# Places of their own for the first block's modulation pieces, and four top-sixteen units under the latents' queries

## The reference

```python
def first_block(x, c, ...):
    c_act = jax.nn.silu(c)
    for l in range(DEPTH):                                   # DEPTH = 2
        mod = c_act @ w_ada[l] + b_ada[l]                    # [1024] @ [1024, 6144]
        sh_m, sc_m, gt_m, sh_f, sc_f, gt_f = jnp.split(mod[:, None, :], N_MOD, axis=-1)
        h = rms_norm(x, g_pre_mix[l]) * (1.0 + sc_m) + sh_m
        y = token_mixer(h, w_in[l], ...)                     # h @ w_in: [256,1024] @ [1024,3656]
        x = x + gt_m * rms_norm(y, g_post_mix[l])
        h = rms_norm(x, g_pre_ffn[l]) * (1.0 + sc_f) + sh_f
        y = conv_glu_ffn(h, w_up_act[l], w_up_lin[l], ...)   # [256,1024] @ [1024,2816], twice
        x = x + gt_f * rms_norm(y, g_post_ffn[l])

def peer(h, w_q, subkeys, u, v):        # 8 heads, 2 halves of 128 keys each, per 128 tokens
    q = (xb @ w_q).reshape(PEER_BLOCK, PEER_HEADS, 2, PEER_DHALF)
    s = jnp.einsum('thpd,hpkd->thpk', q, subkeys)
    s1, i1 = lax.top_k(s[:, :, 0], 16); s2, i2 = lax.top_k(s[:, :, 1], 16)
    cand = s1[..., :, None] + s2[..., None, :]
    top, pos = lax.top_k(cand, 16)
    g = jax.nn.softmax(top, axis=-1)
    ue, ve = u[idx], v[idx]             # a gathered row is 2 x 1024 floats
    act = jax.nn.gelu(jnp.einsum('td,thkd->thk', xb, ue))
    return jnp.einsum('thk,thkd->td', g * act, ve)
```

## Time and profile before

| | us |
|---|---|
| median of 3 runs (lowest to highest) | 3843.72 (3842.69 to 3852.66) |
| profiled execution, its own time | 3842.15 |
| its span, first to last instruction | 3840.9 |
| PE busy | 3050.1 (79%) |
| DVE busy | 2455.0 (64%) |
| ACT, POOL busy | 784.2 (20%), 940.7 (24%) |
| mean granted TensorE clock | 0.909 |
| HBM | 287 GB/s over the span |

### The profile page before, as it was taken

The page is one execution under the profiler, slowest core; times in us unless marked ns, Lnnn a source line. Parts: engine busy times, 40 slices in busy tenths (PEclk is TensorE's granted clock), DMA queues, the critical chain, the costliest instruction groups (busy, mean ns, idle before and its releaser), DMA issues. The chain is left out here.

```text
span 3840.9 us, 28366 instructions
## 1 busy us (share of the span) xinstructions
PE 3050.1 (79%) x8769; PEld 1590.1 (41%) x8769; DVE 2455.0 (64%) x5374; ACT 784.2 (20%) x1876; POOL 940.7 (24%) x842
## 2 busy tenths in 40 slices
PE   6898797899786799787767777777897787777776
PEld 1354464675334377254344223322343462233322
DVE  3224556887677488646656999766514519999665
ACT  1102223232224433225211111100102211111000
POOL 0000001222221233222302344434100013444432
PEclk7999898999898899888879998999996799999999
DMA  6654234999795689966847999999632059999998
GB/s 236 201 178 167 93 114 169 343 356 354 301 356 199 230 349 406 373 248 212 306 154 294 391 388 389 392 422 422 257 138 103 21 206 367 386 389 376 422 421 348
DMA packets 194025, 1102.15 MB, mean 287 GB/s; under 512 B 22517, under 2 KB 22849, under 8 KB 95569
## 3 DMA queue, kind: packets, MB, share of 16 engines
q0 software_dynamic: 114512, 818.87, 54.1%
q1 hardware_dynamic: 78736, 280.90, 20.2%
q10 hardware_dynamic: 624, 0.57, 0.1%
HBM read 1099.18 MB, written 1.05 MB: 286 GB/s over the span
## 5 line engine op out<-in xcount | busy, mean ns | idle before, releaser
L2022 PE MATMUL PS<-AR 128*128 128x512 f32 x2464 | 1216.7, 639 | 400.7 <-DVE AR L2064 341.2
L2121 POOL DMA_INDIRECT AR<-in_uv,AR x768 | 866.1, 1128 | 1641.9 <-PE PS L2022 1142.8
L2069 DVE CUSTOM_DVE_ANT_0 AR<-AR 128x1024 f32<-128x1024 f32 x768 | 935.6, 1220 | 297.2 <-DMA AR<-in_uv,AR 296.7
L2022 PEld LDWEIGHTS PS<-AR 128*128 128x128 f32 x2464 | 476.1, 202 | 1103.3 <-DVE AR L2064 536.5
L694 PE MATMUL PS<-AR 128*128 128x512 f32 (+3 forms) x1304 | 565.3, 588 | 27.4 <-DMA AR<-in_w_in 14.7
L2034 ACT ACTIVATE AR<-AR 128x2 f32<-128x2 f32 x384 | 78.1, 203 | 1514.8 <-DVE AR L2069 1509.2
L694 PEld LDWEIGHTS PS<-AR 128*128 128x128 f32 x1304 | 250.5, 205 | 314.9 <-issue 269.5
L991 PE MATMUL PS<-AR 128*128 128x256 f32 x1408 | 327.2, 392 | 22.9 <-DMA AR<-in_w_up_act 11.9
L326 DVE SCALAR_TENSOR_TENSOR AR<-AR,CC 128x512 f32<-128x512 f32 x280 | 210.5, 752 | 208.5 <-DMA AR<-in_w_ada 130.7
L991 PEld LDWEIGHTS PS<-AR 128*128 128x128 f32 x1408 | 273.2, 196 | 85.0 <-issue 17.4
L1941 PE MATMUL PS<-AR 128*128 128x256 f32 x768 | 186.7, 406 | 26.7 <-DMA AR<-in_peer_w_q 19.6
(11 more groups left out here) (226 smaller groups left out, 2490.3 us busy)
## 6 DMA issues: line engine op xcount, KB each, us to landing
AR<-in_w_mod SPq DMA_DIRECT2D x96, 512.0 KB, 4.3
AR<-in_w_ada SPq DMA_DIRECT2D x96, 512.0 KB, 4.6
AR<-in_w_in SPq DMA_DIRECT2D x56, 512.0 KB, 4.0
AR<-in_peer_w_q SPq DMA_DIRECT2D x48, 512.0 KB, 3.3
AR<-in_w_up_act SPq DMA_DIRECT2D x44, 512.0 KB, 7.7
AR<-in_w_up_lin SPq DMA_DIRECT2D x44, 512.0 KB, 7.5
AR<-in_w_down SPq DMA_DIRECT2D x44, 512.0 KB, 9.6
AR<-in_even_w_in SPq DMA_DIRECT2D x24, 512.0 KB, 4.2
```

What stands on the lines that cost most here:

```text
L2022: ins = pe.eng.matmul(acc[i][hh], e.dg(x), e.buf(x)[:, 1024 + 512 * hh:1536 + 512 * hh], start=(x == e.on[False][i][0]), stop=(x == e.on[F ...
L2069: v.eng.tensor_tensor_reduce(e.buf(x)[:, 0:1024], e.buf(x)[:, 0:1024], norm2(e).H[e.tiles[x // 128]], 1.0, 0.0, ALU.mult, ALU.add, DT[x // ...
L2121: g.eng.indirect_dma_start(e.buf(x), None, D["uv"][e.l], bass.IndirectOffsetOnAxis(ap=idx_at(x // 16, x % 16, 1), axis=0)).then_inc(*land. ...
```

## The change

Three lists of places are added: `OWN_T`, three of 128x512 in the area `t`; `OWN_BIG`, three in `big`; `ACM`, two in `acc`. With `own` given, `Mods` loads each 128x512 half by a DMA of its own (256 KB) into the next of the three places; the DMA waits for DVE's use of the half that lay there, and the first three wait for the `guard`, which is the turned norm that has read the area before. The three modulations named above get `own`. `more` sums in `ACM` in place of `ACW`. For the latents' experts, `ready` no longer holds `more`, and `begin, under` go from 11, 1 to 3, 4.

```diff
+        OWN_T = [T[:, a:a + 512] for a in (1536, 3072, 3584)]
+        OWN_BIG = [BIG[:, 5632 + 512 * i:6144 + 512 * i] for i in range(3)]
+        ACM = [area("acc")[:, 512 * i:512 * i + 512] for i in range(2)]
...
             def sp(self, sp):
+                place, n = {}, len(self.own)
                 for j, hh, outs in self.halves:
                     r = 2 * j + hh
                     for kh in range(4):
-                        load(sp, ("raw", self.key, j, hh, kh), self.w[r, kh].rearrange("p (c n) -> p c n", c=2),
-                             2, 512, [("piece", self.key, j, hh, kh)])
+                        if n:
+                            for c in range(2):
+                                i = self.nth(j, hh, kh, c) % n
+                                sp.wait_ge(place.get(i, self.guard))
+                                sp.eng.dma_start(self.own[i], self.w[r, kh, :, 512 * c:512 * c + 512]).then_inc(
+                                    *land.landed(f"own{i}", "raw", self.key, j, hh, kh, c))
+                                place[i] = ("piece", self.key, j, hh, kh, c)
+                        else:
+                            load(sp, ("raw", self.key, j, hh, kh), self.w[r, kh].rearrange("p (c n) -> p c n", c=2),
+                                 2, 512, [("piece", self.key, j, hh, kh)])
                         yield
...
+                        wt = self.columns(j, hh, kh, c)
+                        v.wait_ge(v.last, ("raw", self.key, j, hh, kh, c) if self.own else ("raw", self.key, j, hh, kh))
...
-                mods_of["first", 0] = ada("ada0b", 0, (2, 4, 3, 5), AF, {0: n1r, 1: n1r}, n1t)
+                mods_of["first", 0] = ada("ada0b", 0, (2, 4, 3, 5), AF, {0: n1r, 1: n1r}, n1t, OWN_T)
...
-                mods_of["next", 0] = ada("ada1a", 1, (1, 0, 2), AF, {0: n2r, 1: n2r, 2: [("added", 0, 2)]}, n2t)
+                mods_of["next", 0] = ada("ada1a", 1, (1, 0, 2), AF, {0: n2r, 1: n2r, 2: [("added", 0, 2)]}, n2t, OWN_BIG)
...
-                                         (0, [(1, 0, "shift", None), (2, 4, "shift", None)])], ACW,
+                                         (0, [(1, 0, "shift", None), (2, 4, "shift", None)])], ACM,
...
-                          mods.finished() + [("sum", before, 255)], 11, 1)
-                  for l, mods, before in ((0, more, "c"), (1, mods_of["odd"], "l0"))]
+                          [("sum", before, 255)] + mods, 3, 4)
+                  for l, mods, before in ((0, [], "c"), (1, mods_of["odd"].finished(), "l0"))]
```

More of the change, by code:

```diff
@@ L262, in program, with __init__ @@
         class Mods:
-            def __init__(self, key, w, row0, jobs, accs, frees, guard=(), every=1):
+            def __init__(self, key, w, row0, jobs, accs, frees, guard=(), every=1, own=()):
+                self.own = own
                 self.key, self.row0, self.jobs, self.accs = key, row0, jobs, accs
@@ L283, in sp, with nth, columns @@
                     for kh in range(4):
-                        load(sp, ("raw", self.key, j, hh, kh), self.w[r, kh].rearrange("p (c n) -> p c n", c=2),
-                             2, 512, [("piece", self.key, j, hh, kh)])
+                        if n:
[8 more added lines that the diff above has]
+                                 2, 512, [("piece", self.key, j, hh, kh)])
                         yield
                 yield
+            def nth(self, j, hh, kh, c):
+                return 8 * [h[:2] for h in self.halves].index((j, hh)) + 2 * kh + c
+            def columns(self, j, hh, kh, c):
+                if self.own:
+                    return self.own[self.nth(j, hh, kh, c) % len(self.own)]
+                return raw_view(2, 512, "raw", self.key, j, hh, kh)[:, c, :]
             def pool(self, g):
@@ L312, in piece @@
                 j, hh, outs = self.halves[q]
-                wt = raw_view(2, 512, "raw", self.key, j, hh, kh)
                 for n, (ci, dst, kind, gain) in enumerate(outs):
@@ L320, in piece @@
                             ("acc", self.key, j, hh, n) if c == 1 and kh == 3 else ())
-                        v.wait_ge(v.last, ("raw", self.key, j, hh, kh))
+                        if self.own:
+                            end = ("piece", self.key, j, hh, kh, c)
+                        wt = self.columns(j, hh, kh, c)
+                        v.wait_ge(v.last, ("raw", self.key, j, hh, kh, c) if self.own else ("raw", self.key, j, hh, kh))
                         if kc == 0:
                             v.wait_ge(("silu",), self.acc_before(q, n))
-                            v.eng.tensor_scalar(acc, wt[:, c, :], col, None, ALU.mult).then_inc(*v.done(*end))
+                            v.eng.tensor_scalar(acc, wt, col, None, ALU.mult).then_inc(*v.done(*end))
                         else:
-                            v.eng.scalar_tensor_tensor(out=acc, in0=wt[:, c, :], scalar=col, in1=acc, op0=ALU.mult,
+                            v.eng.scalar_tensor_tensor(out=acc, in0=wt, scalar=col, in1=acc, op0=ALU.mult,
                                                        op1=ALU.add).then_inc(*v.done(*end))
@@ L358, in out_pe @@
                         bk = bank(pe, SIDE, *key)
-                        pe.wait_ge(("piece", self.key, j, hh, 3), ("acc", self.key, j, hh, n)
+                        pe.wait_ge(("piece", self.key, j, hh, 3, 1) if self.own else ("piece", self.key, j, hh, 3), ("acc", self.key, j, hh, n)
                                    if n < len(outs) - 1 else None)
@@ L857, in ada_rows, with ada @@
                     4: (1, "scale", D["g_pre_ffn"][l]), 3: (0, "shift", None), 5: (3, "gate", D["g_post_ffn"][l])}[j]
-        def ada(key, l, js, accs, frees, guard=()):
-            return Mods(key, D["w_ada"][l], 12 * l, [(j, [(0, *ada_rows(j, l))]) for j in js], accs, frees, guard)
+        def ada(key, l, js, accs, frees, guard=(), own=()):
+            return Mods(key, D["w_ada"][l], 12 * l, [(j, [(0, *ada_rows(j, l))]) for j in js], accs, frees, guard,
+                        own=own)
         def rope(v, x1, x2, c, s, r):
@@ L2458, in program @@
             if l == 0:
-                mods_of["first", 0] = ada("ada0b", 0, (2, 4, 3, 5), AF, {0: n1r, 1: n1r}, n1t)
+                mods_of["first", 0] = ada("ada0b", 0, (2, 4, 3, 5), AF, {0: n1r, 1: n1r}, n1t, OWN_T)
             else:
-                mods_of["first", 1] = ada("ada1b", 1, (4, 3, 5), AF, {0: n1r, 1: n1r, 3: [("added", 0, 3)]}, n1t)
+                mods_of["first", 1] = ada("ada1b", 1, (4, 3, 5), AF, {0: n1r, 1: n1r, 3: [("added", 0, 3)]}, n1t, OWN_T)
             n2 = norm_of["f", l, 2] = Norm(("f", l, 2), HF, LAT, [0, 1], lat_rows, mods_of["first", l],
```

## The result

| kernel | median us, runs | ratio to before, 95% interval | in us |
|---|---|---|---|
| before | 3851.95, 15 | | |
| changed | 3867.08, 15 | 1.0047 [1.0033, 1.0062] | +18 |

The two medians themselves lie 15.1 apart, and the one of before is 8.2 above the 3843.72 that the forecast started from. Of the 35.5 us between the two traces about half is therefore no difference of the kernels, and one trace of each can't tell which half.

A forecast was written before the change was run, and what follows sets the result against it. PE was taken to set the pace in layer 0's projections, DVE in the latents' experts. Terms 5.0 + 2.2 + 0 - 6 - 8.0 = -6.8 gave a median of 3836.9 us; range for 8 in 10, 3820 to 3856.

The forecast's parts named there:

- layer 1's projections: Layer 1: without the ring's older reader `w_in` goes earlier; 8.6 us won less 2.6 for the guard, -6.
- the feed-forward: Layer 0: weights asked for earlier against weights standing on SP behind halves; the two effects taken as equal, 0.
- guard at layer 0's start: Start of layer 0's projections: `even_w_in` stands behind the guarded half, PE starts 6.4 us late, 1.40 given back; +5.0.
- rest of its projections, with the flush: End of layer 0's pieces: with three places the last halves and DVE's sums end later, near 403.0; +2.2 us.
- latents' experts, both stages: Latents' experts: 27 rows go at 2.499 us in place of 2.725, first dot later; -4.0 each, -8.0 together.
- The guard of this stage: Start of layer 0's feed-forward: 0.7 us issues plus 5.6 landing less 3.72 work, 2.6, within the next wait of at most 2.8.
- Rival C: SP stands behind its own halves: feed-forward +18 us, layer 1 nothing; +17.2 in all, 3861 us; chance 0.10.
- the sign named for it: Layer 0's projections: PE's first L694 on the context's weights starts at about 118.5, not 112.1, waiting for `in_even_w_in`.
- the delay of the first dot: Latents' experts: three more units and a late second exponential put the first dot at 2072.7, 2.1 us later.
- B: The ring caused all waits for the first block's weights, so all 32.7 us go: -33.5, 3810 us; chance 0.15.
- D: Latents' experts: first rows land early and gathers set the pace from the start: -15.6, 3828 us; chance 0.10.
- E: Latents' experts gain nothing, exponentials late or dots unmoved; the 8.0 us are lost: +1.2, 3845 us; chance 0.10.

The follow-up runs named there:

- after_again: The changed kernel run once more, unchanged, for a second trace; one execution, 3868.85 us.
- own_only: Changed kernel without the latents' part: three guarded own places for the pieces, latents as before; 1.0077 to before, +30 us.
- own_proj: Against before: three own guarded places in both layers' projections only, ring in the feed-forward, latents as before; 1.0055, +21 us.
- own_ffn: Against before: three own guarded places in layer 0's feed-forward only, ring in both projections, latents as before; 1.0053, +20 us.
- before_again: The kernel before run once more, unchanged, for a second trace; one execution, 3843.84 us.
- experts_only: Changed kernel without the own places: the latents' part alone, pieces in the ring as before; 0.9965 to before, -13 us.
- own3_free: Pieces' places alone, latents as before: three places of 256 KB halves in area ht, which needs no guard; 1.0055 to before, +21 us.
- all7_free: Changed kernel, both parts, with seven places in place of three, the first four not guarded; 0.9899 to before, -39 us, median 3809.98 us.

## Why the prediction was wrong

The time, 3867.1, lies above the range, and the side was wrong: I forecast -6.8 and gave slower a tenth. Of the 30.2 us between 3836.9 and 3867.1, 8.2 are the base, whose median was 3851.95 this time. Two steps failed: layer 1's projections, taken as won, and the feed-forward, put at 0. Step by step, with the measured sizes as the mean of the four traces with three guarded places (changed, after_again, own_only, own_proj, or own_ffn for the feed-forward) less that of the traces with the ring there (before, before_again, experts_only, own_ffn or own_proj):

| term | forecast | measured |
|---|---|---|
| guard at layer 0's start | +5.0 | +7.0 |
| rest of its projections, with the flush | +2.2 | +4.3 |
| layer 0's feed-forward | 0 | +8.9 |
| layer 1's projections | -6 | +11.2 |
| latents' experts, both stages | -8.0 | -11 to -13 |

The measured terms add to 19 or 20, against 18 by the ratio.

- **Layer 1's projections, -6**, is the step that failed most. I took from one row that a ring place's older reader was the gate, and priced what would be won if it went. The new wait was read as one on "the first half", some 1.5 us earlier than before. In fact each of a step's two halves waits for DVE's use three halves back, through a landing of 6 us, so SyncE stood 46 + 12 times for DVE between 640 and 1200 us, and PE's waits for `w_in` are 20 to 22 us where the ring has 13 to 16. The same stretch by the table's measure, one trace each: with three unguarded places -0.2 us (own3_free), with four -7.9, with seven -13.4, where the ring has -2.7 in the mean and three guarded places +8.5; `w_in`'s waits go from 20.9 (own_only) over 17.2 and 9.7 to 8.3. So the gain that I took was there to be had, from four places on, and of the 11.2 lost with three guarded ones 8.7, by that one trace, goes with the guard (4.7 between the two kernels with seven places), which I had priced at 2.6.
- **Layer 0's feed-forward, 0.** The text had a quantity of the right kind, weights let go late through DVE, 4.8 us in its row, and ate it up with the 4.73 wait at 729.14. That wait is no cushion: it is another weight's lateness, and that weight stands on the same queue. The guard of this stage was eaten in the same way, as 2.6 within a wait of 2.8; it is a wait of 7.3 to 9.1, since the weight behind it took 13.0 us and not 5.6 until PE could go on. Rival C said so, with +18 for the stage; it measured +16 in the traces, of which 8 to 10 are the light trace, and +20 by own_ffn's median. Its point of decision (DVE less than one landing ahead of PE) was met and the row for it, 3.6 us, stood in the text. I argued it away with the next chunk's 3.72. That C's total, +17.2, is so near to the measured +18 is luck in part: it had layer 1 at 0 and the experts at -8.0, where 11.2 and -11 to -13 were found.
- **The guard at the start** had nearly its size for a reason that was wrong: it is not `even_w_in` that comes late but the context's norm, behind DVE's wait for the first two halves. I had taken the copy at 112.27 for one of the guarded norm. So the sign named for it, L694 at 118.5 with a wait for `in_even_w_in`, did not come: it starts at 115.14 with no such wait.
- **The flush**: right, PE's wait grew by 2.3 where 2.2 was forecast. The +4.3 of its row in the table holds more than that; what else is open.
- **The experts**: right in mechanism; 27 rows go at 2.504 in place of 2.725 and make 6.0, as worked out, and the 108 others were 0.021 each faster than the 135 (2.704), 2.3 more; the delay of the first dot was 1.6 for 2.1. That makes 6.7 for layer 0's stage, where its row has 5.4 to 6.4 and I had 4.
- **The rivals.** B's price for the full gain of depth was 33.5 less; all7_free gives 39 less, though not by the same terms: its experts' stages gain 12.1 by the trace in place of 8.0, and 11.7 us of PE's waits for the three weights are left, where B's sum had none. D didn't occur: the dots' spacing is 2.7 from the first on. E fell with experts_only.
- **The base.** A sum against a trace that was 10 us short in the stage in dispute starts from too light a stage in any case; but a before that is heavier makes the change look better, so it doesn't explain that -6.8 came out as +18.

Left open: why own_ffn and own_proj together lose more than own_only, why the feed-forward's loss is 8.9 by the traces and 20 by own_ffn's median, and how much of the loss between 131 and 654 us (where DVE and ACT, not SyncE, end PE's waits) is the pieces'. No kernel had the guard of one stage alone.

## What to carry to other kernels

A private buffer for a stream takes its waits out of the shared ring, but not out of the shared queue: whatever issues the DMA stands behind the reader, so count the places against one whole loop, a landing and the reader's turn. Here three places, which gave one half per 3.2 us where the steps want one per 2.7, were too few, and four were enough; that was 43 us. A guard on a buffer's first use is paid by everything behind it on the queue, so put the first loads where nothing lay: with seven places that was worth 15 us.
A wait in one trace is not a cushion for another lateness on the same queue.

## What the runs showed of the hardware that was not expected

- The feed-forward with its pieces in the ring took 10 us more in three further traces (before_again, experts_only and own_proj: +10.3, +10.0, +11.2) than in the one of before, with the waits for its weights at 24 to 26 us in place of 18.0.
- A weight of 512 KB issued at 672.19, right behind two guarded halves, let PE go on only 13.0 us later; the same weight, issued ahead of the stage, had landed after 3.3 us (628.37 to 631.68) in before.
- Halving the size of a DMA (256 in place of 512 KB, 160 in place of 80) had no cost that these runs can see, which is some 13 us: 0.9914 and 0.9912.
- Moving the issue of the halves to GpSimd, with seven places, costs 27 us against SyncE's, though it took away all of PE's waits for those weights.
